# The norm's gain and bias applied to the residual by GpSimd instead of VectorE, at six of seven norms

## The chip, the cores and the metric

The kernel runs on one core of a Trainium2 chip. The metric is device time in microseconds (us) of one execution, as the median over runs. The engines are TensorE (PE, its weight loads PEld), VectorE (DVE), ScalarE (ACT), GpSimd (POOL) and SyncE (SP, which here only starts transfers). All arithmetic is in float32.

## The reference

A first block (gated linear attention, latent attention, a mixture of 64 experts) gives x, of 256 tokens by 1024 features. The change lies in the second block, of two layers, and in the final norm of the first one:

```python
def layer_norm(x, g, b):
    xf = x.astype(jnp.float32)
    mu = jnp.mean(xf, -1, keepdims=True)
    var = jnp.mean(jnp.square(xf - mu), -1, keepdims=True)
    y = (xf - mu) * lax.rsqrt(var + LN_EPS)
    return (y * g.astype(jnp.float32) + b.astype(jnp.float32)).astype(x.dtype)

def second_block(x, mem, ln_g, ln_b, ...):
    alpha = DEEPNORM_ALPHA
    for l in range(DEPTH_2):                      # 2 layers
        x = layer_norm(alpha * x + 0.5 * swiglu(x, ffn_w_gate[l, 0], ffn_w_up[l, 0], ffn_w_down[l, 0]),
                       ln_g[l, 0], ln_b[l, 0])
        ...                                       # u = x @ w_in; tok = short conv (l = 0) or mLSTM (l = 1)
        xa = memory_cross_attention(u[..., -D_XA:], mem_kv)
        mix = jnp.concatenate([tok, xa], -1) @ w_out[l]
        x = layer_norm(alpha * x + mix, ln_g[l, 1], ln_b[l, 1])
        x = layer_norm(alpha * x + 0.5 * swiglu(x, ffn_w_gate[l, 1], ffn_w_up[l, 1], ffn_w_down[l, 1]),
                       ln_g[l, 2], ln_b[l, 2])
    return x
```

So there are seven norms in a row: norm 0 is the RMS norm at the end of the first block (a gain, no bias), norms 1 to 6 are the layer norms (gain g and bias b, each a row of 1024).

## The kernel before

The second block runs as FFN 0, conv, FFN 1, FFN 2, lstm, FFN 3; FFN n works on the result of norm 0, 2, 3 and 5, `conv` on that of norm 1, `lstm` on that of norm 4, and norm 6 ends the kernel. The residual h lies in SBUF as `c_h`: 128 partitions (tokens) by 2 tiles by 1024 features. Each engine runs a program written out by hand, in the order of its functions, and waits for the others by semaphores; there is no scheduler. SyncE loads the weights in 1 MB pieces into a ring of 8 (`x_ring`).

At norm j, VectorE adds the new products from PSUM to h (`sums` L1678, or `merged` L1722 to L1769), takes the statistics, and `scaled(j, t)` (L1684 to L1687; for norm 0 L2040 to L2043) turns tile t of h into (h - mean) / root in place, in two halves of 512 columns, each counted on the semaphore `zn`. TensorE then transposes the tile (`turn`, L1256, semaphore `turned`, four counts a norm), and `spread` moves it from PSUM to `xT`, features by tokens: VectorE does half (L1695, L1697), ScalarE the other (L1563, L1565). The gain and bias are applied there, per feature, as scalars; so TensorE's operand `xT` needs nothing from what follows.

The residual itself also needs gain and bias before the next norm adds to it. `rows(j)` does this on h in place: for each tile a product with `n_g` (L1708; L1711 at norm 0) and, from norm 1 on, an addition of `x_b` (L1709), each 128x1024. `n_g` and `x_b` hold the rows g and b in all partitions; ScalarE's queue reloads them (`load_rows(j)`) behind the semaphore `rows`, at the start of `conv` and `lstm` and in the third step of each FFN. In an FFN VectorE calls `rows(j)` behind `hidden(0)`, the first of 11 steps; in `conv` and `lstm` it is its first work.

An FFN on VectorE starts with `token_sums` (L1802 to L1806): four combinations of quarters of `xT`, all in SBUF. TensorE, which has meanwhile multiplied the plain products of two steps (`plain(0)`, then `turn(j, 1)`, then `plain(1)`), waits for them before `mixed(0)`:

```python
                turn(j, 0)
                ...
                plain(0)
                turn(j, 1)
                plain(1)
                pe.wait_ge(s["tx"], n + 1)
                mixed(0)
```

GpSimd builds constants at the start of the kernel, masks the attention and multiplies a gate (L827) before 101 us, and then works only in `lstm`: two masks and, at L2064, the product of the output gate `x_og` with `x_hg`, two instructions of 128x768.

Of the kernel before, what the change touches and what calls it, by code (L numbers as in the profile page):

```python
# [8 lines left out]
ALU = mybir.AluOpType  # L9
# [7 lines left out]
TT = S // P  # L17
# [1151 lines left out]
def whole(K, M, E, N, X, Y, out):  # L1169
# [38 lines left out]
    with nc.Block() as block:  # L1208
# [459 lines left out]
        def _(v):  # L1668
            c = lambda i: K.vc(v, i)

            def sums(j, t, scale, last):
                for m in range(2):
                    if 2 * t + m < 3:
                        v.wait_ge(s["bank"], BANK_AT[j] + 2 * t + m + 1)
                    else:
                        v.wait_ge(s["spent"], last)
                    hm = h[:, t, m * 512:(m + 1) * 512]
                    c(v.scalar_tensor_tensor(out=hm, in0=yb(t, m), scalar=scale, in1=hm, op0=ALU.mult, op1=ALU.add))  # L1678
                    c(v.bn_stats(N.stats[:, t, m, :], hm))
                v.bn_aggr(N.mv[:, t, :], N.stats[:, t, :, :]).then_inc(s["mv"], 1)  # L1680
# [30 lines left out]
                        v.tensor_tensor(h[:, t, :], h[:, t, :], N.g[:, :], ALU.mult).then_inc(s["rows"], 1)  # L1711

            def norm(j, scale, last):
                sums(j, 0, scale, last)
                scaled(j, 0)
                sums(j, 1, scale, last)
                spread(j, 0)
                scaled(j, 1)
                spread(j, 1)

            def merged(n, j, scale, last):
                add = lambda t, m, x: K.vc.mark(v.scalar_tensor_tensor(out=h[:, t, m * 512:(m + 1) * 512], in0=x, scalar=scale,  # L1722
                                                                       in1=h[:, t, m * 512:(m + 1) * 512], op0=ALU.mult, op1=ALU.add))
                after = lambda n: v.wait_ge(K.vc.sem, n)
                got = lambda n: v.wait_ge(s["bank"], BANK_AT[j] + n)
                prod = lambda p: ps[:, DB[p], :]
                stats = lambda t, m: v.bn_stats(N.stats[:, t, m, :], h[:, t, m * 512:(m + 1) * 512])
                both = lambda o, x, y: K.vc.mark(v.tensor_tensor(N.ud[:, o, :], x, y, ALU.add))
                v.wait_ge(s["kept"], (NFC + 1) * (n + 1))
                x = add(0, 0, N.pd[:, :])  # L1730
                got(2)
                after(x)
                c(add_last(0, 0, prod(2), scale))
                stats(0, 0)
                got(3)
                u2 = both(0, N.pd[:, :], prod(6))
                got(4)
                after(u2)
                u4 = both(1, N.ud[:, 0, :], prod(5))
                y = add(1, 0, N.ud[:, 0, :])  # L1740
                after(u4)
                x = add(0, 1, N.ud[:, 1, :])
                z = add(1, 1, N.ud[:, 1, :])
                got(5)
                after(x)
                c(add_last(0, 1, prod(3), scale))
                c(stats(0, 1))
                v.bn_aggr(N.mv[:, 0, :], N.stats[:, 0, :, :]).then_inc(s["mv"], 1)
                got(6)
                after(z)  # L1750
                z = add(1, 1, prod(7))
                scaled(j, 0)
                y = add(1, 0, prod(7))
                after(z)
                stats(1, 1)
                v.wait_ge(s["spent"], last)
                after(y)
                c(add_last(1, 0, prod(4), scale))
                c(stats(1, 0))
                v.bn_aggr(N.mv[:, 1, :], N.stats[:, 1, :, :]).then_inc(s["mv"], 1)  # L1760
                if j < 6:
                    spread(j, 0)
                scaled(j, 1)
                if j < 6:
                    spread(j, 1)
# [42 lines left out]
            def ffn(n, j):  # L1808
                at = AT_FFN[n]

                def post(cc):
                    v.wait_ge(s["spent"], at + 2 * cc + 2)
                    if n or cc:
                        v.wait_ge(s["post"], NFC * n + cc)
                    if cc >= 2:
                        v.wait_ge(s["act"], NFC * n + cc - 1)
                        v.wait_ge(s["hid"], NFC * n + cc - 1)
                    base = 4 if cc % 2 == 0 else 0
                    prod = lambda p: ps[:, base + GU[p][0], GU[p][1]:GU[p][1] + 256].rearrange("p (w t) -> p w t", w=2)
                    u = lambda i: N.us[:, i, :, :]  # L1820
                    o = lambda f2, t: N.cb[:, cc % 2, 2 * f2 + t, :, :]
                    v.wait_ge(s["kept"], (NFC + 1) * n + cc + 1)
                    one = N.p1[:, cc % 2, :, :]
                    u2 = K.vc.mark(v.tensor_tensor(u(0), one, prod(6), ALU.add))  # L1824
                    v.tensor_tensor(o(0, 0), one, prod(2), ALU.add)
                    v.wait_ge(K.vc.sem, u2)
                    u3 = K.vc.mark(v.tensor_tensor(u(1), u(0), prod(7), ALU.add))
                    u4 = K.vc.mark(v.tensor_tensor(u(2), u(0), prod(5), ALU.add))
                    v.wait_ge(K.vc.sem, u3)
                    v.tensor_tensor(o(1, 1), u(1), prod(5), ALU.add)  # L1830
                    v.wait_ge(K.vc.sem, u4)
                    v.tensor_tensor(o(0, 1), u(2), prod(3), ALU.add)
                    v.tensor_tensor(o(1, 0), u(1), prod(4), ALU.add).then_inc(s["post"], 1)

                def hidden(cc):
                    v.wait_ge(s["act"], NFC * n + cc + 1)
                    v.tensor_tensor(N.hT[:, cc, :, :], N.act[:, cc % 2, :, :], N.cb[:, cc % 2, :, 1, :], ALU.mult).then_inc(s["hid"], 1)

                def hidden_sums(cc):
                    v.wait_ge(s["hid"], NFC * n + cc + 1)  # L1840
                    if cc >= 4:
                        v.wait_ge(s["spent"], at + 2 * NFC + cc - 3)
                    o, x = N.hs[:, cc % 4], N.hT[:, cc]
                    first = K.vc.mark(v.tensor_tensor(o[:, 0], x[:, 1], x[:, 3], ALU.add))
                    v.tensor_tensor(o[:, 2], x[:, 0], x[:, 1], ALU.subtract)
                    v.wait_ge(K.vc.sem, first)
                    c(v.tensor_tensor(o[:, 1], o[:, 0], x[:, 0], ALU.subtract))
                    v.tensor_tensor(o[:, 3], x[:, 2], o[:, 1], ALU.subtract).then_inc(s["hsum"], 1)

                token_sums(n, j)  # L1850
                weight_sums(n, 2)
                weight_sums(n, 3)
                for cc in range(NFC):
                    post(cc)
                    weight_sums(n, 2 * cc + 4)
                    weight_sums(n, 2 * cc + 5)
                    hidden(cc)
                    if cc == 0:
                        rows(j)
                    if cc >= NFC - 2:  # L1860
                        for m in range(2):
                            hidden_sums(2 * (cc - NFC + 2) + m)
                for cc in range(4, NFC):
                    weight_sums(n, 2 * NFC + cc)
                    hidden_sums(cc)
                if n == 1:
                    weight_sums(2, 0)
                    weight_sums(2, 1)
                merged(n, j + 1, 0.5 / ALPHA, at + FPOS)
# [22 lines left out]

            def conv():
                at = AT_CONV
                rows(1)
                c(v.memset(X.pad[:, :, 0:QE], 0.0))
                queries(0, 0, at)

# [29 lines left out]

            def lstm():
                at = AT_LSTM  # L1930
                rows(4)
                queries(1, 1, at)
                v.memset(X.va[:, :, :, HD:HD + 1], 1.0)
                for hh in range(HH):
# [119 lines left out]
        @block.gpsimd  # L2054
        def _(g):
            front.gpsimd(g)
            g.wait_ge(ls["wt"], TT * HH)
            g.affine_select(out=X.wt[:, 0, :, 0:P], in_=X.wt[:, 0, :, 0:P], compare_op=ALU.is_ge, fill=0.0, base=0,
                            pattern=[[0, HH], [1, P]], channel_multiplier=-1).then_inc(ls["masked"], 1)
            g.affine_select(out=X.wt[:, 1, :, P:S], in_=X.wt[:, 1, :, P:S], compare_op=ALU.is_ge, fill=0.0, base=0,  # L2060
                            pattern=[[0, HH], [1, P]], channel_multiplier=-1).then_inc(ls["masked"], 1)
            g.wait_ge(ls["og"], 3)
            for t in range(TT):
                i = g.tensor_tensor(X.og[:, t, :], X.og[:, t, :], X.hg[:, :], ALU.mult)  # L2064
            i.then_inc(ls["ogg"], 1)


def place(nc, into, prefix, at, end, **shapes):
# [138 lines left out]
```

## Time and profile before

| | |
|---|---|
| median of 3 runs | 2252.16 us (2251.8 to 2252.19) |
| profiled execution | 2251.79 us, of which span 2249.9 us |
| TensorE busy | 1843.9 us, 82% |
| VectorE busy | 859.9 us, 38%, 1804 instructions |
| ScalarE busy | 214.2 us, 10% |
| GpSimd busy | 17.9 us, 1%, 41 instructions |

The span is the time between the first and the last record of the profiled execution; the device time is a little longer. The first 1113 us are the first block and the experts; the second block is what follows. PEclk is the clock granted to TensorE as a share of 2.4 GHz: 1.00 is that level and 0.50 is 1.2 GHz.

### The profile page before, as it was taken

How to read it: one execution, taken by the hardware profiler on the slowest of the kernel's cores; microseconds unless marked ns; L12 is line 12 of the kernel's file. 1: busy time of each engine (PE TensorE's matmuls, PEld its weight loads, DVE VectorE, ACT ScalarE, POOL GpSimd, SP SyncE). 2: the span in 40 equal slices, each digit the busy share in tenths (PEclk: the TensorE clock that was granted, in tenths of full speed). 3: DMA queues.
4: the chain of work that ended last, by engine and by line, in shares of the span. 5: the costliest groups of instructions: out<-in, count | busy, mean ns of one | idle time of the engine just before them, and what ended most of it. 6: DMA issues, size and time to landing. Idle time of an engine off the chain costs nothing.

```text
span 2249.9 us, 26172 instructions
## 1 busy us (share of the span) xinstructions
PE 1843.9 (82%) x11372; PEld 1225.0 (54%) x11372; DVE 859.9 (38%) x1804; ACT 214.2 (10%) x409; POOL 17.9 (1%) x41
## 2 busy tenths in 40 slices
PE   8997665566665556656699999999999999989997
PEld 6754232222222222212399658699579947859973
DVE  2223111111011111110276742476776755347675
ACT  2321000000000000000100011000010002201000
POOL 1100000000000000000000000000000000000000
PEclk9998887888887888777899999999999999999999
DMA  9268999999999999999955443365545444315540
GB/s 275 71 244 346 427 427 428 427 428 428 428 424 428 427 428 428 428 428 427 361 173 182 174 160 122 118 200 184 172 150 180 177 150 150 113 59 185 181 186 27
DMA packets 185419, 604.64 MB, mean 269 GB/s; under 512 B 17805, under 2 KB 139079, under 8 KB 161239
## 3 DMA queue, kind: packets, MB, share of 16 engines
q1 hardware_dynamic: 179680, 595.51, 68.4%
q10 hardware_dynamic: 5623, 7.42, 1.0%
q8 instruction: 92, 1.51, 0.3%
q14 instruction: 24, 0.20, 0.0%
HBM read 601.86 MB, written 1.05 MB: 268 GB/s over the span
## 4 chain that ended last, share of the span: by engine, by line
PE 62%; DMA 30%; SPq 3%; DVE 3%; issue 1%; ACT 1%; ACTq 0%; DVEq 0%
PE banks L1280 24%; PE banks L1307 11%; DMA e_W<-in_expert_w_up 10%; DMA e_W<-in_expert_w_down 10%; DMA e_W<-in_expert_w_gate 9%; PE banks L907 6%; PE banks L1355 5%; PE banks L915 3%; PE banks L1399 2%; PE banks L1475 2%; PE banks L203 2%; SPq L144 1%; SPq L887 1%; DMA x_ring<-in_ffn_w_up 1%; PE banks L398 1%
## 5 line engine op out<-in xcount | busy, mean ns | idle before, releaser
L907 PE MATMUL banks<-e_W,e_xT 128*32 128x512 f32 x2048 | 284.8, 716 | 176.5 <-DMA e_W<-in_expert_w_up 87.6
L907 PEld LDWEIGHTS banks<-e_W,e_xT 128*32 128x32 f32 x2048 | 79.4, 129 | 370.0 <-issue 368.7
L915 PE MATMUL banks<-e_W,e_hT 128*32 128x512 f32 x960 | 139.2, 745 | 140.0 <-DMA e_W<-in_expert_w_down 140.0
L1280 PE MATMUL banks<-x_xs,x_sums 128*128 128x128 f32 x2112 | 243.0, 275 | 0.0
L1280 PEld LDWEIGHTS banks<-x_xs,x_sums 128*128 128x128 f32 x2112 | 239.4, 192 | 0.0
L1280 PE MATMUL banks<-x_xT,x_ring 128*128 128x128 f32 x1408 | 169.0, 280 | 8.5 <-DVE x_xT L1695 6.8
L1280 PEld LDWEIGHTS banks<-x_xT,x_ring 128*128 128x128 f32 x1408 | 164.9, 196 | 9.5 <-DVE x_xT L1695 7.5
L915 PEld LDWEIGHTS banks<-e_W,e_hT 128*32 128x32 f32 x960 | 38.2, 133 | 230.3 <-issue 230.3
L1083 DVE TENSOR_TENSOR c_h<-c_h,banks 128x1024 f32<-128x1024 f32 x32 | 39.0, 1221 | 312.3 <-PE banks L935 312.3
L1307 PE MATMUL banks<-x_sums,x_hs 128*128 128x512 f32 x264 | 125.0, 592 | 0.0
L1355 PE MATMUL banks<-x_xT,x_ring 128*128 128x256 f32 x544 | 122.0, 386 | 1.6 <-DVE x_xT L1695 1.6
L1079 DVE TENSOR_TENSOR e_xT<-banks,e_fng 128x512 f32<-128x512 f32 x32 | 20.6, 686 | 255.5 <-PE banks L895 255.5
L1355 PEld LDWEIGHTS banks<-x_xT,x_ring 128*128 128x128 f32 x544 | 104.7, 194 | 17.4 <-DVE x_xT L1695 1.9
L1107 DVE TENSOR_TENSOR e_hid<-e_act,banks 128x512 f32<-128x512 f32 x16 | 11.0, 688 | 234.7 <-PE banks L907 234.7
L1280 PE MATMUL banks<-x_xT,x_sums 128*128 128x128 f32 x704 | 86.2, 276 | 2.6 <-DVE x_xs L1806 2.6
L1280 PE MATMUL banks<-x_xs,x_ring 128*128 128x128 f32 x704 | 85.8, 275 | 0.0
L1307 PEld LDWEIGHTS banks<-x_sums,x_hs 128*128 128x128 f32 x264 | 50.2, 190 | 63.1 <-issue 63.1
L1280 PEld LDWEIGHTS banks<-x_xT,x_sums 128*128 128x128 f32 x704 | 82.1, 192 | 3.4 <-DVE x_xs L1806 3.4
L1280 PEld LDWEIGHTS banks<-x_xs,x_ring 128*128 128x128 f32 x704 | 82.1, 192 | 0.0
L1307 PE MATMUL banks<-x_ring,x_hT 128*128 128x512 f32 x176 | 81.4, 592 | 0.0
L1824 DVE TENSOR_TENSOR x_us<-x_p,banks 128x256 f32<-128x256 f32 x44 | 18.5, 421 | 156.3 <-PE banks L1280 156.3
L935 PE MATMUL banks<-e_y,e_mixT 128*128 128x512 f32 x128 | 59.2, 605 | 18.3 <-ACT e_y L1048 17.1
(466 smaller groups left out, 2027.5 us busy)
## 6 DMA issues: line engine op xcount, KB each, us to landing
e_W<-in_expert_w_gate SPq DMA_DIRECT2D x64, 2048.0 KB, 21.7
e_W<-in_expert_w_up SPq DMA_DIRECT2D x64, 2048.0 KB, 20.7
e_W<-in_expert_w_down SPq DMA_DIRECT2D x64, 2048.0 KB, 20.2
x_ring<-in_ffn_w_gate SPq DMA_DIRECT2D x44, 1024.0 KB, 5.4
x_ring<-in_ffn_w_up SPq DMA_DIRECT2D x44, 1024.0 KB, 7.6
x_ring<-in_ffn_w_down SPq DMA_DIRECT2D x44, 1024.0 KB, 5.1
x_ring<-in_w_in_mlstm SPq DMA_DIRECT2D x13, 1024.0 KB, 5.2
x_ring<-in_w_in_conv SPq DMA_DIRECT2D x10, 1024.0 KB, 5.2
```

The lines of the kernel that those rows point to most:

```text
L144: sp.dma_start(dst, src).then_inc(ld["params"], 16)
L203: i = pe.matmul(o, lhs(k), rhs(k), start=(k == 0), stop=(k == KD - 1))
L398: pe.matmul(ps[:, 4 + 2 * t + n, :], M.yT[:, k, t * P:(t + 1) * P], K.wout[:, k, n * 512:(n + 1) * 512], start=(k == 0), stop=False)
L907: i = pe.matmul(ps[SLOT * j:SLOT * (j + 1), b, :], E.xT[:, x, k, SLOT * j:SLOT * (j + 1)], E.W[:, slot0 + j, k * DE:(k + 1) * DE], start=( ...
L915: i = pe.matmul(ps[SLOT * j:SLOT * (j + 1), 2 + c, :], E.hT[:, f, SLOT * j:SLOT * (j + 1)], E.W[:, slot0 + j, f * D + c * 512:f * D + (c + ...
L935: i = pe.matmul(ps[:, 6 - 2 * t + c, :], E.mixT[:, x, t, :], E.y[:, c * 512:(c + 1) * 512], start=True, stop=True)
L1083: return v.tensor_tensor(K.h[:, t, :], K.h[:, t, :], ps[:, 6 - 2 * t:8 - 2 * t, :].rearrange("p b n -> p (b n)"), ALU.add)
L1280: mm = pe.matmul(ps[:, bank, lo + which * P:lo + (which + 1) * P], a, b, start=(k == 0), stop=(k == 3))
L1307: mm = pe.matmul(ps[:, DB[p], :], a, b, start=(c == 0), stop=(c == NFC - 1))
L1355: mm = pe.matmul(ps[:, bank, f2 * S:(f2 + 1) * S], w8(i)[:, k, f2 * P:(f2 + 1) * P], N.xT[:, k, :], start=(k == 0), stop=(k == KD - 1))
L1399: mm = pe.matmul(yb(t, m), X.mixT[:, 2 * kk + k2, t * P:(t + 1) * P], w2(at + n)[:, k2, m * 512:(m + 1) * 512], start=(n == 0 and k2 == 0) ...
L1475: mm = pe.matmul(ps[:, bank, t * FC:(t + 1) * FC], N.xT[:, k, t * P:(t + 1) * P], w8(i)[:, k, :], start=(k == 0), stop=(k == KD - 1))
```

## The change

The function `rows(j)` of norms 0 to 5 moves from VectorE's program to GpSimd's. VectorE keeps only `rows(6)`. GpSimd runs `rows(0)` to `rows(4)` one after the other behind its last instruction of the first block, each tile as soon as `turned` says that both its halves are transposed and `ld_rows` that g and b are there; then the masks and the product of `lstm`; then `rows(5)`. A chain semaphore (`p_chain`) stands between product and addition of a tile. VectorE waits for the semaphore `rows` before its first addition of the next norm.

```diff
--- before.py
+++ after.py
@@ -1711,6 +1711,7 @@
                         v.tensor_tensor(h[:, t, :], h[:, t, :], N.g[:, :], ALU.mult).then_inc(s["rows"], 1)
 
             def norm(j, scale, last):
+                v.wait_ge(s["rows"], TT * j)
                 sums(j, 0, scale, last)
                 scaled(j, 0)
                 sums(j, 1, scale, last)
@@ -1727,6 +1728,7 @@
                 stats = lambda t, m: v.bn_stats(N.stats[:, t, m, :], h[:, t, m * 512:(m + 1) * 512])
                 both = lambda o, x, y: K.vc.mark(v.tensor_tensor(N.ud[:, o, :], x, y, ALU.add))
                 v.wait_ge(s["kept"], (NFC + 1) * (n + 1))
+                v.wait_ge(s["rows"], TT * j)
                 x = add(0, 0, N.pd[:, :])
                 got(2)
                 after(x)
@@ -1855,8 +1857,6 @@
                     weight_sums(n, 2 * cc + 4)
                     weight_sums(n, 2 * cc + 5)
                     hidden(cc)
-                    if cc == 0:
-                        rows(j)
                     if cc >= NFC - 2:
                         for m in range(2):
                             hidden_sums(2 * (cc - NFC + 2) + m)
@@ -1892,7 +1892,6 @@
 
             def conv():
                 at = AT_CONV
-                rows(1)
                 c(v.memset(X.pad[:, :, 0:QE], 0.0))
                 queries(0, 0, at)
 
@@ -1928,7 +1927,6 @@
 
             def lstm():
                 at = AT_LSTM
-                rows(4)
                 queries(1, 1, at)
                 v.memset(X.va[:, :, :, HD:HD + 1], 1.0)
                 for hh in range(HH):
@@ -2054,6 +2052,19 @@
         @block.gpsimd
         def _(g):
             front.gpsimd(g)
+
+            def rows(j):
+                g.wait_ge(moe.ld_rows, 16 + 32 * j)
+                for t in range(TT):
+                    g.wait_ge(s["turned"], 4 * j + 2 * t + 2)
+                    if j:
+                        K.pc(g, g.tensor_tensor(h[:, t, :], h[:, t, :], N.g[:, :], ALU.mult))
+                        g.tensor_tensor(h[:, t, :], h[:, t, :], N.b[:, :], ALU.add).then_inc(s["rows"], 1)
+                    else:
+                        g.tensor_tensor(h[:, t, :], h[:, t, :], N.g[:, :], ALU.mult).then_inc(s["rows"], 1)
+
+            for j in range(5):
+                rows(j)
             g.wait_ge(ls["wt"], TT * HH)
             g.affine_select(out=X.wt[:, 0, :, 0:P], in_=X.wt[:, 0, :, 0:P], compare_op=ALU.is_ge, fill=0.0, base=0,
                             pattern=[[0, HH], [1, P]], channel_multiplier=-1).then_inc(ls["masked"], 1)
@@ -2063,6 +2074,7 @@
             for t in range(TT):
                 i = g.tensor_tensor(X.og[:, t, :], X.og[:, t, :], X.hg[:, :], ALU.mult)
             i.then_inc(ls["ogg"], 1)
+            rows(5)
 
 
 def place(nc, into, prefix, at, end, **shapes):
```

On VectorE at the start of `conv` (`c_h` is the residual, `n_g` and `x_b` the rows of gain and bias, `n_lnT` the parameters by feature) stood, after norm 1's scaling of tile 1:

```order
L1684 RECIPROCAL n_root<-n_root 128x1
L1687 TENSOR_SCALAR c_h<-c_h,n_mv,n_root 128x512 x2
L1695 TENSOR_SCALAR x_xT<-banks,n_lnT 128x128 x4
L1708 TENSOR_TENSOR c_h<-c_h,n_g 128x1024
L1709 TENSOR_TENSOR c_h<-c_h,x_b 128x1024
L1708 TENSOR_TENSOR c_h<-c_h,n_g 128x1024
L1709 TENSOR_TENSOR c_h<-c_h,x_b 128x1024
L1896 MEMSET x_pad 128x12x3
L1874 COPY x_qx<-banks 64x2x256
```

and now stands:

```order
L1684 RECIPROCAL n_root<-n_root 128x1
L1687 TENSOR_SCALAR c_h<-c_h,n_mv,n_root 128x512 x2
L1695 TENSOR_SCALAR x_xT<-banks,n_lnT 128x128 x4
L1895 MEMSET x_pad 128x12x3
L1874 COPY x_qx<-banks 64x2x256
```

The four instructions on h are gone from VectorE; the order of the others is the same.

On GpSimd (`r_e` and `r_off` are constants of the router, the last work of the first block; the part in brackets is what an instruction waits for) the new instructions stand between that and the masks of `lstm`; these are the first rows of the new piece, those of norms 0 and 1, and norms 2 to 4 repeat the last four:

```order
L835 CAST r_e_187<-r_e32i 128x64 [waits p_chain]
L836 TENSOR_SCALAR r_off<-r_e_187 128x64 [waits p_chain]
L2064 TENSOR_TENSOR c_h<-c_h,n_g 128x1024 [waits s_turned,e_ld_rows]
L2064 TENSOR_TENSOR c_h<-c_h,n_g 128x1024 [waits s_turned]
L2061 TENSOR_TENSOR c_h<-c_h,n_g 128x1024 [waits s_turned,e_ld_rows]
L2062 TENSOR_TENSOR c_h<-c_h,x_b 128x1024 [waits p_chain]
L2061 TENSOR_TENSOR c_h<-c_h,n_g 128x1024 [waits s_turned]
L2062 TENSOR_TENSOR c_h<-c_h,x_b 128x1024 [waits p_chain]
```

GpSimd has 22 more instructions (67 rows where there were 45), and nothing of its own stands ahead of them between norms.

## Rows read from the trace of the kernel before

**Rows 1.** The page: busy time, share of the span and instructions of TensorE

```profile
PE 1843.9 (82%) x11372; PEld 1225.0 (54%) x11372; DVE 859.9 (38%) x1804; ACT 214.2 (10%) x409; POOL 17.9 (1%) x41
```

**Rows 2.** The chain that ended last, FFN 0: start us, us, what

```profile
1126.56 130.69 PE banks L1280 x1168
...
1257.25 63.53 PE banks L1307 x148
```

**Rows 3.** The products of `rows` on VectorE, one line: count, min/median/max ns, forms

```profile
L1708 DVE TENSOR_TENSOR c_h<-c_h,n_g x12: 1211/1218/1220, 1329.3 to 2244.4; 128x1024 f32<-128x1024 f32 x12
```

**Rows 4.** Busy time in a stretch of FFN 2; engine, us busy (instructions), clock, DMA

```profile
1672.00:1688.00 16.00, 16.00 (x145) 16.00 (x145) 15.83 (x27) 1.65 (x3) 0.00 (x0) 1.00 0.72 230
```

**Rows 5.** Timeline at norm 1 and the start of `conv`

```profile
1324.26 1.50 ACT L1563 ACTIVATE x_xT<-banks,n_lnT 128x128 f32<-128x128 f32 x4 [4.03 <-PE banks L1256]
...
1326.70 1.00 DVE L1687 TENSOR_SCALAR c_h<-c_h,n_mv,n_root 128x512 f32<-128x512 f32 x2
...
1330.06 23.76 PE L1355 MATMUL banks<-x_xT,x_ring 128*128 128x256 f32 x96 [1.64 <-DVE x_xT L1695]
```

**Rows 6.** GpSimd and VectorE at 1991.7 us in the LSTM, and line L2017

```profile
1991.71 1.80 POOL L2064 TENSOR_TENSOR x_og<-x_og,x_hg 128x768 f32<-128x768 f32 x1
...
1991.76 1.87 DVE L2017 TENSOR_SCALAR x_pad<-x_pad,x_hmv,x_hrs 128x192 f32<-128x192 f32 x1
...
L2017 DVE TENSOR_SCALAR x_pad<-x_pad,x_hmv,x_hrs x8: 366/368/1871, 1991.8 to 1995.3; 128x192 f32<-128x192 f32 x8
```

**Rows 7.** Timeline at 94 to 98 us: start, us, engine, line, operation

```profile
94.83 1.89 POOL L827 TENSOR_TENSOR q_rg<-q_rg,w_gg 128x1024 f32<-128x1024 f32 x1 [14.54 <-ACT q_rg L531]
...
95.64 0.42 DVE L664 TENSOR_TENSOR q_st<-q_st,banks 128x256 f32<-128x256 f32 x1
...
96.10 0.90 DVE L665 TENSOR_TENSOR q_st<-q_st,w_dec 128x256 f32<-128x256 f32 x1
...
97.49 0.43 DVE L665 TENSOR_TENSOR q_st<-q_st,w_dec 128x256 f32<-128x256 f32 x1
```

**Rows 8.** Timeline at the start of FFN 0

```profile
1113.38 0.88 DVE L2043 TENSOR_SCALAR c_h<-c_h,n_root 128x512 f32<-128x512 f32 x2
...
1113.68 1.14 ACT L1565 ACTIVATE x_xT<-banks,n_lnT 128x128 f32<-128x128 f32 x4 [0.54 <-PE banks L1256]
...
1115.35 6.38 PE L1280 MATMUL banks<-x_xT,x_ring 128*128 128x128 f32 x32 [1.71 <-DVE x_xT L1697]
...
1122.64 0.37 ACT L1565 ACTIVATE x_xT<-banks,n_lnT 128x128 f32<-128x128 f32 x1 [7.81 <-PE banks L1256]
...
1123.88 0.69 DVE L1802 TENSOR_TENSOR x_xs<-x_xT 128x512 f32<-128x512 f32 x1 [0.56 <-ACT x_xT L1565]
```

**Rows 9.** Timeline at the start of FFN 2

```profile
1649.02 1.50 ACT L1563 ACTIVATE x_xT<-banks,n_lnT 128x128 f32<-128x128 f32 x4 [4.03 <-PE banks L1256]
...
1651.42 3.84 PE L1280 MATMUL banks<-x_xT,x_ring 128*128 128x128 f32 x32 [2.44 <-DVE x_xT L1695]
...
1651.47 1.00 DVE L1687 TENSOR_SCALAR c_h<-c_h,n_mv,n_root 128x512 f32<-128x512 f32 x2
...
1656.17 1.51 ACT L1563 ACTIVATE x_xT<-banks,n_lnT 128x128 f32<-128x128 f32 x4 [5.46 <-PE banks L1256]
...
1657.78 0.69 DVE L1802 TENSOR_TENSOR x_xs<-x_xT 128x512 f32<-128x512 f32 x1 [0.68 <-ACT x_xT L1563]
...
1658.39 0.68 DVE L1803 TENSOR_TENSOR x_xs<-x_xT 128x512 f32<-128x512 f32 x1
...
1660.45 2.05 PE L1280 MATMUL banks<-x_xT,x_sums 128*128 128x128 f32 x16 [0.75 <-DVE x_xs L1806]
```

**Rows 10.** Busy time and granted clock around norm 1 and in FFN 2

```profile
1323.00:1330.00 7.00, 2.33 (x17) 1.63 (x15) 6.60 (x17) 3.19 (x9) 0.00 (x0) 0.92 1.07 342
...
1330.00:1333.00 3.00, 2.94 (x7) 2.44 (x8) 2.93 (x4) 0.00 (x0) 0.00 (x0) 0.50 0.79 246
...
1655.50:1660.40 4.90, 4.21 (x38) 4.01 (x36) 3.95 (x9) 3.45 (x7) 0.00 (x0) 1.00 0.36 111
```

## The prediction

> **What bounds the kernel now.** I read the page first: TensorE is busy 82% of the span [rows 1]. Then the chain of waits. In the part that the change touches (from 1113 us, after the expert layer) it consists of long unbroken runs of matmuls: one FFN is 130.69 us of products at L1280 and 63.53 us at L1307, with nothing between [rows 2]. Only at the norms does the chain leave TensorE, for a few microseconds each: additions, scaling, transposes, the spread into xT, and `token_sums`. The question is therefore whether the 22 moved instructions lie on these short crossings or under the long runs, before and after.
>
> **What the change removes: nothing from the path.** VectorE loses 22 instructions of about 1.22 us [rows 3], 26.8 us of busy time. Those of norms 0, 2, 3 and 5 stood behind `hidden(0)`, inside an FFN. In FFN 2's stretch around them TensorE is busy 16.00 of 16.00 us while VectorE is also nearly full (15.83) [rows 4]; the other three FFNs read the same. VectorE is full there, but TensorE does not wait for it, so an earlier VectorE is worth 0. Those of norms 1 and 4 stood at the head of `conv` and `lstm`, in the time in which TensorE works on its first 96 matmuls (23.76 us from 1330.06 [rows 5]); again 0. If the cover were gone, each norm would be worth 4 x 1.22 = 4.9 us, but no row shows TensorE waiting for them.
>
> **The new wait is free.** `rows(j)` must be done before norm j+1's first addition. GpSimd needs some 10 us from the transposes; the next addition is far behind that: an FFN is 194 us, and the first 96 matmuls of `conv` alone are 23.76 us [rows 2, 5]. ScalarE's reload of g and b waits for GpSimd too, ahead of `conv` and `lstm`, but its next work is after the second or later group of matmuls. 0 us.
>
> **What the change adds: GpSimd on the path of VectorE.** On GpSimd, one product of two real 128x768 operands took 1.80 us [rows 6]. In proportion 128x1024 is 1.80 x 1024/768 = 2.40 us. The lower bound is the 1.89 us of L827 on 128x1024, whose second operand repeats one column per block [rows 7]; I take 2.40, because both operands of the moved work are full rows.
> [...]
>
> More important is when it runs. Before, the instructions stood deep in the FFN. Now GpSimd has nothing else to do and starts as soon as the transposes of a tile are done, which is when ScalarE's spread starts. That is exactly the crossing. And these two rows show that the engines exclude each other:
> - L2017 on VectorE, one SBUF operand into SBUF, normally 0.368 us, took 1.871 us: it began at 1991.76 beside the GpSimd product of 1991.71 to 1993.51, and ended at 1993.63, 0.12 us after it [rows 6].
> - L665, two SBUF operands, took 0.90 instead of 0.43 us beside the GpSimd product of 94.83 to 96.72, and ended at 97.00. L664, with one operand in PSUM, ran beside the same product in its normal 0.42 us [rows 7].
>
> So VectorE's SBUF-only instructions stand still until GpSimd's ends; those that read PSUM don't. A stopped one ends 0.12 to 0.28 us after the release (192 and 256 elements; 0.55 us for 512, by proportion of the second).
> The Trainium skill (SBUF — State Buffer, section "SBUF: two separate sides") calls it an exclusive lock held for a whole instruction by whichever began first; the trace agrees in both rows. It does not say who is next when GpSimd waits and VectorE has its next instruction ready; that is the choice below.
>
> Now each crossing. The SBUF-only instructions of VectorE there are `scaled` (L1687, L2043) and `token_sums` (L1802 to L1806).
> 1. **FFN 0, second tile's scaling.** Tile 0 is transposed at 1113.68. L2043's two halves of tile 1 run 1113.38 to 1114.26 in the order of the program ahead of the spread [rows 8]. GpSimd's product takes the port behind the first of them (about 1113.9) and ends at 1116.3; the second half ends at 1116.5 instead of 1114.26: **+2.3 us**, and all of it is on the path, since the spread and TensorE's start at 1115.35 stand behind it.
> 2. **conv and lstm, tile 1's scaling.** Tile 0's product starts at 1324.3 and ends at 1326.7, as L1687 begins (1326.70). Whoever gets the port first, GpSimd's addition (2.40 us) goes ahead of at least the second half, and the tile's transposes, its spread and the matmuls at 1330.06 stand behind both halves [rows 5]. **+2.3 us**, and the same in the norm ahead of `lstm`, whose rows repeat this pattern: together +4.6. Tile 1's two GpSimd instructions end before VectorE next needs SBUF alone.
> 3. **Tile 1's scaling in FFN 1, 2, 3: hidden.** In FFN 2 tile 0 is transposed at 1649.02, the product runs 1649.1 to 1651.5, L1687 starts at 1651.47, the addition goes between its halves to 1654.4. The transposes that need it come behind the first 32 matmuls, which end at 1655.26 [rows 9]. They are the cover; 0 us, with under a microsecond to spare.
> 4. **`token_sums` behind tile 1's product.** FFN 2: tile 1 is transposed at 1656.17, the product ends at 1658.6. L1802 is ready at 1657.78 and ends at 1659.15 instead of 1658.47: +0.7, and TensorE's 1660.45 waits for these four [rows 9]. Three such FFNs: **+2.1**. FFN 0: transposed at 1122.64, product to 1125.0, L1802 ready at 1123.88, +1.0 [rows 8]. Together **+3.1**.
> 5. **`token_sums` behind tile 1's addition.** GpSimd asks for the port again 0.1 to 0.2 us later, while L1802 runs. If it gets it next, L1803 stands still for 2.4 us. FFN 1, 2, 3: **+7.2**; FFN 0 has no addition.
>
> Sum: 2.3 + 4.6 + 3.1 + 7.2 = **17.2 us**.
>
> **The clock.** After the gaps around the transposes at 1323 to 1330 us (TensorE busy 2.33 of 7.00) the granted clock is 0.50, the 1.2 GHz level, for 3 us [rows 10]. The price of such a fall is in the first 32 matmuls of an FFN: 6.38 us in FFN 0, which starts behind a like gap, and 3.84 us in FFN 2 [rows 8, 9], so 2.5 us. At FFN 2's `token_sums` TensorE is busy 4.21 of 4.90 us and the clock stays at 1.00, the 2.4 GHz level [rows 10]. With 3 us more idle there, each of four such places may fall: 0 to 10.2 us. I take one, 2.5 us.
>
> **Forecast.** 17.2 + 2.5 = 19.7 us, on the profiled execution's 2251.79 us (span 2249.9 and 1.9 around it), which is 0.4 under the median 2252.16: **2272 us**, 0.9% slower.
>
> **Rivals.**
> - *VectorE keeps the port while its next instruction is ready* (not slower). Records of back-to-back VectorE instructions overlap by 0.08 us (L1802 runs 1657.78 to 1658.47, L1803 starts at 1658.39) [rows 9], so the port may never come free between them. Then items 1, 2 and 5 vanish and only item 4 is left: +3.1 us, 2255.3 us. It decides at the first L2043 pair. For it: these overlaps. Against: L1805 and L1806 wait for a semaphore of the instruction before them. 0.15. A difference under 0.2% (4.5 us) is what a measurement of this kernel can't tell from no change, so this counts as the same.
> - *Every collision and every fall of the clock*: 17.2 + 10.2 = 27.4 us, 2280 us. For it: each lengthened gap resembles the one at 1323 us. 0.12.
> - *No cost*: GpSimd wakes late enough to miss the crossings, or the norm waits for something else meanwhile; 2252 us. It would have to wake over 7 us late (from 1649.0 past 1655.3 or from 1656.2 past `token_sums`), and nothing in the trace shows such a delay. 0.05.
> - *Faster*: VectorE's 4.9 us per FFN free TensorE after all. It would need a TensorE wait there, and [rows 4] has none; one FFN's worth of it would give 2247 us. 0.03.
> - The forecast with no, one or two falls of the clock: 0.65.
>
> **Range and chances.** The forecast and the second rival are slower, 0.77; the first rival plus a single fall of the clock would also pass 4.5 us, so slower 0.79, same 0.18, faster 0.03. With 1.89 instead of 2.40 us for a GpSimd instruction, the sum is some 5 us smaller (0.51 us at each of the ten collisions), which lies in between. The range takes in the first rival's 2255 and reaches past the second's 2280: 2255 to 2282. The forecast's own range is 2266 to 2278.
>
> **What would show it.** GpSimd: 22 more instructions, about 2.4 us, the first at 1113.7. VectorE: single records of L2043, L1687 and the `token_sums` lines of 2 to 3 us; the norm's crossings longer, the FFN runs of 130.69 and 63.53 us unchanged. If all `token_sums` records are 0.69 us except the first, the first rival holds. I would be wrong above all if the lock were won by VectorE each time, or if GpSimd's records themselves grew to several times 2.4 us because they are the ones that wait.

## The result, and the profile after

The changed kernel takes 2275.2 us (median of 4 runs, 2270.92 to 2276.73) against 2252.18 us: ratio 1.0101, 95% interval [1.0088, 1.0113]. It is 23 us slower. The profiled execution took 2273.82 us, with a span of 2272.0 us, 22.1 us over the span before. In what follows one execution of one kernel (GpSimd's work on other data) took 2856.6 us at a mean granted clock of 0.638 and is left out; all others of a kernel lie within 0.2% of its median.

The page of the changed kernel, busy time by engine, to be set beside [rows 1]:

```profile
PE 1850.8 (81%) x11372; PEld 1230.1 (54%) x11372; DVE 856.9 (38%) x1782; ACT 214.2 (9%) x409; POOL 70.5 (3%) x63
```

VectorE has lost 22 instructions of 1.22 us, 26.8 us, and yet is busy only 3.0 us less (859.9 before). So its other instructions have records that are some 24 us longer in all. Which ones, the view by line of the changed kernel says (count, then min/median/max ns):

```profile
L2041 DVE TENSOR_SCALAR c_h<-c_h,n_root x4: 479/486/2642, 1112.0 to 1113.8; 128x512 f32<-128x512 f32 x4
...
L1687 DVE TENSOR_SCALAR c_h<-c_h,n_mv,n_root x24: 535/545/2715, 1324.1 to 2263.6; 128x512 f32<-128x512 f32 x24
...
L1804 DVE TENSOR_TENSOR x_xs<-x_xT x4: 1341/1344/1703, 1125.3 to 2056.7; 128x512 f32<-128x512 f32 x4
...
L1805 DVE TENSOR_TENSOR x_xs<-x_xT x4: 680/2826/2827, 1127.0 to 2058.0; 128x512 f32<-128x512 f32 x4
...
L1807 DVE TENSOR_TENSOR x_xs<-x_xT,x_xs x4: 678/679/680, 1127.6 to 2060.7; 128x512 f32<-128x512 f32 x4
```

L2041 and L1687 are the scaling, L1804 to L1808 the four instructions of `token_sums` (L1802 to L1806 before). The first of `token_sums` takes at least 1.34 us instead of 0.69 in every FFN, the second 2.83 us in three of four, and the third always its own time. The timeline of the changed kernel at the starts of FFN 0, `conv` and FFN 1 shows why:

```profile
1113.39 3.04 DVE L2041 TENSOR_SCALAR c_h<-c_h,n_root 128x512 f32<-128x512 f32 x2
1113.69 1.14 ACT L1565 ACTIVATE x_xT<-banks,n_lnT 128x128 f32<-128x128 f32 x4 [0.54 <-PE banks L1256]
1113.81 2.34 POOL L2064 TENSOR_TENSOR c_h<-c_h,n_g 128x1024 f32<-128x1024 f32 x1 [1012.89 <-PE banks L1256]
...
1117.52 5.65 PE L1280 MATMUL banks<-x_xT,x_ring 128*128 128x128 f32 x32 [3.87 <-DVE x_xT L1697]
...
1326.82 2.35 POOL L2061 TENSOR_TENSOR c_h<-c_h,n_g 128x1024 f32<-128x1024 f32 x1 [200.34 <-PE banks L1256]
1326.88 0.69 DVE L1728 BATCH_NORM_STATS2 n_stats<-c_h 128x6 f32<-128x512 f32 x1
...
1329.16 3.16 DVE L1687 TENSOR_SCALAR c_h<-c_h,n_mv,n_root 128x512 f32<-128x512 f32 x2
1329.24 2.34 POOL L2062 TENSOR_TENSOR c_h<-c_h,x_b 128x1024 f32<-128x1024 f32 x1
...
1335.53 23.06 PE L1355 MATMUL banks<-x_xT,x_ring 128*128 128x256 f32 x96 [1.64 <-issue]
...
1451.87 2.36 POOL L2061 TENSOR_TENSOR c_h<-c_h,n_g 128x1024 f32<-128x1024 f32 x1 [1.99 <-PE banks L1256]
...
1453.43 1.34 DVE L1804 TENSOR_TENSOR x_xs<-x_xT 128x512 f32<-128x512 f32 x1 [0.68 <-ACT x_xT L1563]
...
1454.30 2.67 POOL L2062 TENSOR_TENSOR c_h<-c_h,x_b 128x1024 f32<-128x1024 f32 x1
1454.70 2.83 DVE L1805 TENSOR_TENSOR x_xs<-x_xT 128x512 f32<-128x512 f32 x1
1457.45 0.68 DVE L1807 TENSOR_TENSOR x_xs<-x_xT,x_xs 128x512 f32<-128x512 f32 x1
...
1458.91 3.48 PE L1280 MATMUL banks<-x_xT,x_sums 128*128 128x128 f32 x16 [3.55 <-DVE x_xs L1808]
```

Read the FFN 1 part slowly. GpSimd's product ends at 1454.23; L1804, ready since 1453.43, ends at 1454.77, 0.54 us later. The addition has asked for the port at 1454.30, and its record is 2.67 us instead of 2.34, since it first waits for L1804. L1805 begins at 1454.70, ends at 1457.53, again 0.56 us behind the addition (1456.97). So each side gets the port (the way to SBUF that the two engines are taken to share) when the other's instruction ends, although VectorE had its next instruction ready. TensorE waits 3.55 us for `token_sums`, against 0.75 before; [rows 9] show the same place in FFN 2. At `conv` the two halves of the scaling take 3.16 instead of 1.00 us together [rows 5], and in FFN 0 3.04 instead of 0.88 [rows 8]. At `conv` it is the first half that is stopped: its record begins at 1329.16, the product ends at 1329.17, the addition runs from 1329.24 to 1331.58, and the first half ends at 1331.87, after 2.71 us. The second half takes its usual time. So the addition went ahead of an instruction whose record had begun 0.08 us earlier.

One line of the `conv` part limits the reading. The statistics (L1728) take their only input from the residual in SBUF and write to SBUF, and yet took their usual 0.69 us in the middle of GpSimd's product (1326.82 to 1329.17). So "SBUF-only" is too wide a name for what stands still: held up here are the scaling and the instructions with two operands in SBUF.

The second cost shows as a lower clock. The chain of the changed kernel has the same long runs as [rows 2], but those of FFN 1, 2 and 3 have grown from 130.69 to 132.32 us:

```profile
1129.02 130.69 PE banks L1280 x1168
1259.71 63.53 PE banks L1307 x148
...
1458.91 132.32 PE banks L1280 x1168
1591.22 63.53 PE banks L1307 x148
```

Windows of the changed kernel around FFN 1's `token_sums` (us, then PE, PEld, DVE, ACT, POOL busy, granted clock, DMA) say that it is the granted clock, which is 1.00 up to the gap and 0.56 behind it:

```profile
1453.50:1458.90 5.40, 1.86 (x17) 1.66 (x15) 5.37 (x5) 1.77 (x3) 3.40 (x2) 1.00 0.00 0
1458.90:1462.00 3.10, 3.09 (x16) 3.10 (x17) 3.07 (x6) 0.00 (x0) 0.00 (x0) 0.56 0.00 0
```

Following the chain of both kernels from crossing to crossing gives the whole account:

| crossing | collision, us | clock, us | shift so far, us |
|---|---|---|---|
| FFN 0: scaling; `token_sums` | 2.2; 1.0 | -0.7 (first 32 matmuls 5.65 instead of 6.38) | 2.5 |
| conv: scaling | 2.3 (see below) | | 4.8 |
| FFN 1: `token_sums` | 2.8 | 1.6 (long run) | 9.2 |
| FFN 2: `token_sums` | 2.8 | 1.6 (first 32, 5.46 instead of 3.84), 1.6 (long run) | 15.3 |
| lstm: scaling | 2.3 | | 17.6 |
| FFN 3: `token_sums` | 2.8 | 1.6 (long run) | 22.1 |

That is 16.2 us of collisions and 5.7 us of clock; rounding hides another 0.2 us. The 2.3 us at `conv` are a net figure: the first half of the scaling ends 2.2 us later, the transposes and the spread behind it take 0.9 us more at a lower clock, and the 96 matmuls win back 0.7 us (23.06 instead of 23.76).

The clock column has two parts that differ in what they prove. The 1.6 us in the long runs of FFN 1, 2 and 3 (4.9 us) stand behind gaps lengthened by `token_sums`, from 0.75 to 3.55 us. The 1.6 us in FFN 2's first 32 matmuls don't: the gap ahead of them is 2.44 us in both kernels. They took 5.47 us, too, in two kernels below that have no collision there and are no slower (`late` and `tail_product`, whose FFN 3 in turn took 3.84 us where the kernel before has 5.47). So this part isn't shown to be the change's doing, and neither is the 0.7 us won back in FFN 0.

### The profile page after: what moved, and what is told of

Read it like the earlier page. It is cut to its first block, busy times and chain, and to the rows that moved or that the text cites. A ratio compares the mean times of both kernels' runs of the same rounds, so it can differ in the third digit from the quotient of the medians.

```text
span 2272.0 us, 26178 instructions
## 1 busy us (share of the span) xinstructions
PE 1850.8 (81%) x11372; PEld 1230.1 (54%) x11372; DVE 856.9 (38%) x1782; ACT 214.2 (9%) x409; POOL 70.5 (3%) x63
## 4 chain that ended last, share of the span: by engine, by line
PE 62%; DMA 30%; DVE 4%; SPq 3%; issue 1%; ACT 1%; ACTq 0%; DVEq 0%
PE banks L1280 24%; PE banks L1307 11%; DMA e_W<-in_expert_w_up 10%; DMA e_W<-in_expert_w_down 10%; DMA e_W<-in_expert_w_gate 9%; PE banks L907 6%; PE banks L1355 5%; PE banks L915 3%; PE banks L1399 2%; PE banks L1475 2%; PE banks L203 2%; SPq L144 1%; SPq L887 1%; DMA x_ring<-in_ffn_w_up 1%; PE banks L398 1%
```

## The experiments

Eight kernels ran. They stand beside runs of the kernel before on the same chip: 2252.0 us (median of 18) for the first four, 2251.69 us (of 33) for the others. Those runs lie between 2249.88 and 2254.28 us, a wider spread than in the result above; part of it comes from ahead of the norms, where nothing differs, since the first scaling starts anywhere from 1110.5 to 1113.8 us in the profiled executions. My theory: VectorE's scaling and its instructions with two operands in SBUF exclude GpSimd's, and are excluded by them, and the change put GpSimd's into the crossings, where VectorE's are on the path. The rivals: GpSimd's work costs in proportion wherever it is; the order and the new semaphores of the residual cost.

**Only tile 0 by GpSimd.** VectorE keeps tile 1 where it was.

```diff
+                for t in (0,):                      # GpSimd's rows(j), j < 6
+                    g.wait_ge(s["turned"], 4 * j + 2 * t + 2)
...
-                for t in range(TT):                 # VectorE's rows(j)
+                for t in (range(TT) if j == 6 else (1,)):
```

> GpSimd takes only tile 0 of each moved norm; VectorE keeps tile 1 at its old place. If each collision is an SBUF-only VectorE instruction standing still behind a GpSimd instruction, only the scaling of tile 1 is hit: 2.2 us in FFN 0 and 2.3 us each at conv and lstm, 6.8 us in all, with 0 to 3 us of clock more or less: 2257 to 2262 us. The records of token_sums are 0.69 us. Rival, that the cost comes from all of GpSimd's work alike (half of it here): +11.5 us, 2263.7 us.

2259.16 us, +7.2 us, ratio 1.0031 [1.0021, 1.0041]. By line:

```profile
L1687 DVE TENSOR_SCALAR c_h<-c_h,n_mv,n_root x24: 535/546/2717, 1319.7 to 2245.5; 128x512 f32<-128x512 f32 x24
...
L1804 DVE TENSOR_TENSOR x_xs<-x_xT x4: 692/694/694, 1122.0 to 2043.0; 128x512 f32<-128x512 f32 x4
```

The scaling is hit and `token_sums` not at all. But only two of the three scalings are hit. In FFN 0 the pair of halves was over at 1112.75, and GpSimd's product began at 1113.00: the transposes of tile 0, which release it, took 1.81 us there, at a granted clock of 0.57, against 1.09 us at 1.00 in the changed kernel. Item 1 is thus a race that, in these two traces, the speed of the transposes decides, by a few tenths of a microsecond. The 7.2 us are two scalings of 2.3 us, 4.6 us, and 2.6 us that these don't account for. The profiled execution, at 2255.77 us, is one of the two shortest of nine (2255.62 to 2261.28) and shows 5.5 us, counted from tile 1's scaling in FFN 0 to the end; whether the race went the other way in the longer ones isn't known.

**Only tile 1 by GpSimd.** The mirror image, with `(1,)` for GpSimd and `(0,)` for VectorE.

> GpSimd takes only tile 1; VectorE keeps tile 0. Port theory: only token_sums are hit, 1.0 us in FFN 0 and 2.8 us in each of FFN 1, 2, 3, 9.4 us; the granted clock falls behind the lengthened gaps, 1.6 us each in three FFNs, 4.9 us: +14.3 us, 2266 us, and every record of the scaling is 0.54 us. The two halves together make the 22 us of the change. Rival, that the halves are alike: +11.5 us each. If the clock falls whatever the gap before token_sums, it is in tile0_only too.

2265.96 us, +14.0 us, ratio 1.0061 [1.0044, 1.0078].

```profile
L1687 DVE TENSOR_SCALAR c_h<-c_h,n_mv,n_root x24: 540/544/549, 1322.3 to 2257.1; 128x512 f32<-128x512 f32 x24
...
L1804 DVE TENSOR_TENSOR x_xs<-x_xT x4: 1404/1408/1779, 1123.5 to 2050.2; 128x512 f32<-128x512 f32 x4
...
L1805 DVE TENSOR_TENSOR x_xs<-x_xT x4: 679/2824/2828, 1125.2 to 2051.5; 128x512 f32<-128x512 f32 x4
```

Every scaling has its own time, and the four `token_sums` are within 0.1 us of the changed kernel's. The three long runs behind them took 132.32, 132.32 and 132.27 us. The same number of GpSimd instructions costs twice what tile 0's do: it is the place that counts, not only the amount. The two halves add up to 21.2 us, against 23 for the change.

**The same work on other data.** VectorE does all rows as before; GpSimd does two-operand instructions of 128x1024 on the memory values, which nobody writes, into a scratch tile.

```diff
+            def other(j):
+                for t in range(TT):
+                    g.wait_ge(s["turned"], 4 * j + 2 * t + 2)
+                    K.pc(g, g.tensor_tensor(X.bin[:, :], mv[:, :], mv[:, :], ALU.mult))
+                    if j:
+                        K.pc(g, g.tensor_tensor(X.bin[:, :], mv[:, :], mv[:, :], ALU.add))
```

> The kernel before, with VectorE still doing all rows, and GpSimd doing two-operand instructions of 128x1024 at the moments of the change on operands that no other engine touches at that time (it reads the memory values, writes a scratch tile in bfloat16; the output is the reference's). Port theory: the crossings are as in the changed kernel, +22 us, 2271 to 2277 us. Rival, that the residual itself (its order, its semaphore, the new waits of VectorE and ScalarE) makes the cost: 2252 us.

2264.31 us (median of three: 2264.18, 2264.31 and, profiled, 2268.42), +12.3 us, ratio 1.0055 [1.0035, 1.0076]. The rival (2252 us) falls: without any change to the residual, its waits or VectorE's program, over half of the loss is there. It is less than the +22 us I expected, and the trace says in part why:

```profile
1327.16 1.90 POOL L2063 TENSOR_TENSOR x_bin<-c_memv 128x1024 bf16<-128x1024 f32 x1 [200.34 <-PE banks L1256]
```

My stand-in takes 1.90 us, not 2.35, so each collision is shorter (the longest scaling 2.06 instead of 2.72 us, the second of `token_sums` 2.37 instead of 2.83). And TensorE's gap at `token_sums` is 2.69 us in FFN 1, 2 and 3 alike, but only FFN 2's long run grew to 132.32 us; the other two kept their 130.69. So what the clock did behind a gap of that length was not always the same.

**The same work later.** In an FFN GpSimd waits for the fourth `hidden`, in `conv` and `lstm` for the spread of both tiles. ScalarE's reload of gain and bias moves with it.

```diff
                     g.wait_ge(s["turned"], 4 * j + 2 * t + 2)
+                    if j in AT_NORM:                 # [0, 2, 3, 5]
+                        g.wait_ge(s["hid"], NFC * AT_NORM.index(j) + 4)
+                    else:
+                        g.wait_ge(s["xt_v"], TT * (j + 1))
+                        g.wait_ge(s["xt_a"], TT * (j + 1))
...
-                    if c == 2:                       # ScalarE, in an FFN
+                    if c == 7:
                         load_rows(j + 1)
```

> The changed kernel, with GpSimd released later: in an FFN behind the fourth hidden, in conv and lstm behind the spread of both tiles; ScalarE's reload of gain and bias in an FFN moves from its third to its eighth step. Port theory: nothing SBUF-only of VectorE on the path collides; inside the FFN TensorE covers: 2252 us, at most +3 if VectorE, held up for up to 9.4 us in each FFN, is late for a product. Rival, that the work on GpSimd costs wherever it stands (waits, memory): still +10 us or more.

2252.65 us, ratio 1.0004 [0.9994, 1.0013]: no difference. All 22 instructions are still GpSimd's. A window of FFN 1 in which its four run, and the scaling by line:

```profile
1500.00:1512.00 12.00, 12.00 (x110) 12.00 (x109) 7.57 (x12) 1.02 (x2) 9.73 (x4) 1.00 0.55 171
```

```profile
L1688 DVE TENSOR_SCALAR c_h<-c_h,n_mv,n_root x24: 539/544/548, 1320.3 to 2240.8; 128x512 f32<-128x512 f32 x24
```

TensorE is busy in 12.00 of 12.00 us beside GpSimd's 9.73. This is the whole change without its place in time. It also agrees with VectorE's 26.8 us being worth nothing, though GpSimd holds VectorE up there too (one L1788 in this FFN took 2.85 us instead of 0.68), so it is no test of their removal alone.

**Only the product by GpSimd.** VectorE adds `x_b` at the old place.

```diff
                     if j:
-                        K.pc(g, g.tensor_tensor(h[:, t, :], h[:, t, :], N.g[:, :], ALU.mult))
-                        g.tensor_tensor(h[:, t, :], h[:, t, :], N.b[:, :], ALU.add).then_inc(s["rows"], 1)
+                        g.tensor_tensor(h[:, t, :], h[:, t, :], N.g[:, :], ALU.mult).then_inc(s["mulled"], 1)
```

> GpSimd makes only the products of norms 0 to 5, at the moments of the change; VectorE makes the additions at their old place. Port theory with GpSimd let in between two VectorE instructions: the scaling in FFN 0 is hit by 2.2 us; at conv and lstm the product ends as the scaling begins, 0 to 0.1 us; token_sums stand behind the product alone, 1.0 us in FFN 0 and 0.65 us in each of the other three. +5.2 us and one clock fall at most: 2257 to 2259 us. Rival, that half the GpSimd work is half the cost: +11 us or more.

2258.38 us, +6.7 us, ratio 1.0026 [1.0017, 1.0035]. At `conv` the tie is as narrow as expected and costs nothing; its timeline:

```profile
1326.29 2.34 POOL L2068 TENSOR_TENSOR c_h<-c_h,n_g 128x1024 f32<-128x1024 f32 x1 [200.34 <-PE banks L1256]
...
1328.63 1.00 DVE L1687 TENSOR_SCALAR c_h<-c_h,n_mv,n_root 128x512 f32<-128x512 f32 x2
```

The product ends at 1328.63, exactly where L1687 begins. Left are FFN 0's scaling and the first of each `token_sums` (1.34 us, 1.71 in FFN 0), 5.1 us in all, and the clock. So most of the change's loss hangs on the ten additions, each of which asks for the port right behind a product. Of the clock, the chain of waits shows two things, in FFN 1 and at FFN 2's start:

```profile
1443.68 5.46 PE banks L1280 x32
...
1454.98 130.69 PE banks L1280 x1168
...
1655.08 5.47 PE banks L1280 x32
```

Behind the less lengthened `token_sums` the long run has its 130.69 us, and so have the other three. But the first 32 matmuls of FFN 1 and FFN 2 lost 1.6 us each (3.84 before), again behind gaps as long as before (2.18 and 2.44 us).

**Writes only.** VectorE does all rows; GpSimd fills a scratch tile, four times a tile of the residual, without reading anything.

```diff
+                    for _ in range(4 if j else 2):
+                        K.pc(g, g.memset(X.bin[:, :], 0.0))
```

> The kernel before, with VectorE doing all rows, and GpSimd writing zeros to a scratch tile (no operand read) at the moments of the change, four writes a tile (two at norm 0). If a GpSimd instruction holds VectorE's second port whatever it does, both the scaling and token_sums have records over their own time, each by up to one write of about 1 us: +5 to 12 us, 2257 to 2264 us. If what is fought over in token_sums is the reading of two operands alone, the token_sums stay at 0.69 us, only the scaling (one operand, 0.54 us) is longer: +1 to +5 us. If only reads collide at all: 2252 us.

2254.63 us, +2.9 us, ratio 1.0012 [1.0003, 1.0022]. By line:

```profile
L1687 DVE TENSOR_SCALAR c_h<-c_h,n_mv,n_root x24: 540/546/1247, 1321.9 to 2245.1; 128x512 f32<-128x512 f32 x24
...
L1802 DVE TENSOR_TENSOR x_xs<-x_xT x4: 691/692/693, 1124.1 to 2042.6; 128x512 f32<-128x512 f32 x4
```

The middle case: a write of GpSimd (about 1 us each) holds up the scaling, which has one operand (up to 1.25 instead of 0.54 us), and leaves `token_sums`, two operands, entirely alone, although a series of four writes (two in FFN 0) runs beside each. The Trainium skill (SBUF — State Buffer, section "SBUF: two separate sides") limits the collision of a two-operand instruction to a GpSimd instruction that reads SBUF; the trace agrees, with 0.693 us as the longest of four.

**The last norm's tile 0 by GpSimd.** Two attempts at a gain: at norm 6 nothing covers VectorE's rows, 4.8 us, behind which only the output's transfer is left. One gives GpSimd product and addition of tile 0, the other the product alone; all else is the kernel before.

```diff
+            g.wait_ge(moe.ld_rows, 16 + 32 * 6)
+            g.wait_ge(s["zn"], 4 * 6 + 2)
+            K.pc(g, g.tensor_tensor(h[:, 0, :], h[:, 0, :], N.g[:, :], ALU.mult))      # tail_both; .then_inc(s["early"], 1) in tail_product
+            g.tensor_tensor(h[:, 0, :], h[:, 0, :], N.b[:, :], ALU.add).then_inc(s["early"], 1)   # tail_both only
```

> The kernel before, but at the last norm alone GpSimd does product and addition of tile 0 while VectorE is busy with tile 1; VectorE does tile 1 as before. Before, VectorE's four instructions at the end took 4.7 us of the path. GpSimd starts behind tile 0's scaling, 4.7 us before the end of its addition; the second half of tile 1's scaling stands still for about 0.6 us; two instructions (2.4 us) leave the end: 1.7 us faster, about 2250.4 us against 2252.1. Rival: the transfer of tile 0 or GpSimd's addition is late, and nothing is gained.

> The kernel before, but at the last norm GpSimd makes only the product of tile 0, in the time in which VectorE still works from PSUM; it ends before the scaling of tile 1. Nothing collides and one VectorE instruction of 1.2 us leaves the end: 1.2 us faster, about 2250.9 us against 2252.1.

2251.53 us, ratio 0.9998 [0.9989, 1.0007], and 2250.65 us, ratio 0.9995 [0.9986, 1.0004], against 2251.69 us. Neither can be told from no change by the measured times. The timelines of the end can tell more; first product and addition (span 2251.0), then the product alone (span 2248.5):

```profile
2242.26 2.34 POOL L2069 TENSOR_TENSOR c_h<-c_h,x_b 128x1024 f32<-128x1024 f32 x1
...
2243.01 2.33 DVE L1687 TENSOR_SCALAR c_h<-c_h,n_mv,n_root 128x512 f32<-128x512 f32 x2
```

```profile
2237.70 2.35 POOL L2071 TENSOR_TENSOR c_h<-c_h,n_g 128x1024 f32<-128x1024 f32 x1 [243.26 <-DVE c_h L1687]
...
2240.87 1.00 DVE L1687 TENSOR_SCALAR c_h<-c_h,n_mv,n_root 128x512 f32<-128x512 f32 x2
```

From the start of tile 1's scaling to the end of the span it is 8.0 us with both, 7.6 us with the product alone, and 8.85 us before. With both, the addition holds up both halves of the scaling (2.33 instead of 1.00 us), where I had expected 0.6 us for the second half alone, and over half of the 2.4 us saved is lost again. The product alone fits beside instructions that read PSUM and the statistics, and its 1.2 us are saved in full. It is the best version of this study by its trace, at a gain below what the runs resolve.

## Why the prediction was right

- **What is removed is worth 0**: right as far as the traces show. In the changed kernel no long run and no crossing is shorter for it, and `late`, which has the same instructions off VectorE, is no faster.
- **The new wait is free**: right. VectorE's first addition of a norm is never released by GpSimd. At the FFNs it waits for ScalarE's copy `x_pd` in both kernels, idle 24.9 us in four times, and behind `conv` and `lstm` for TensorE, 1.19 and 1.83 us against 1.11 and 1.75 before.
- **GpSimd's instruction, 2.40 us**: measured 2.34 to 2.36 where it isn't itself held up. The Trainium skill (GPSIMD Engine Reference, section on performance versus the Vector engine) gives 4497 ns for an addition of 2048 elements; half of it, an estimate of 2.25 us, is a little low.
- **Items 1, 2 and 3**: 2.2 us measured for 2.3 in FFN 0; 2.3 each for 2.3 at `conv` and `lstm`; hidden in FFN 1 to 3 as said (the two halves of L1687 take 3.04 us at 1447.12 and TensorE's matmuls behind 1447.07 run on). Two things I had not said: item 1 depends on how fast tile 0's transposes run and fell away in `tile0_only`; and at `conv` the addition went ahead of both halves, where I had it at least ahead of the second.
- **Items 4 and 5**: 1.0 for 1.0 in FFN 0; 2.8 for 3.1 (0.7 + 2.4) in the other three. In FFN 1 the addition ends 2.20 us behind L1804 where I had 2.40 us of standing still, and the stopped L1805 then ends 0.56 us behind it instead of needing its full 0.68.
- **Who gets the port**: GpSimd, in each case, between two VectorE instructions. The first rival (VectorE keeps it, 2255 us) is refuted by every L1805 of 2.83 us and by `tile1_only`. Sum of the collisions 16.2 us for 17.2.
- **Which instructions stand still**: the rule "SBUF-only" was too wide. The statistics (L1728) were not held up. They are on the path at `conv` but were not in the sum, so nothing in it changed.
- **The clock**: this term was mis-sized. I took one fall of 2.5 us among the four `token_sums`. There were three, in FFN 1, 2 and 3, of 1.6 us each; the sign that I named, FFN runs unchanged at 130.69 us, failed in three of four. The price was too high, since I had read it from a stretch that began at 0.50, and the number too low. Another 1.6 us at FFN 2's start and the 0.7 us won back at FFN 0 come from places that I hadn't in the term. In all it is 5.7 us for 2.5.
- **The sum**: its two errors, -1.0 and +3.2 us, have opposite signs, and by that luck the total (22.1 us for 19.7, the last 0.2 is rounding) came nearer than the clock term did. The measured median is 3 us above the forecast, with the four executions of the changed kernel 5.8 us apart. One figure of a rival was off, with nothing resting on it: to wake at 1655.3 instead of 1649.0 is 6.3 us late, not over 7.
- **What a measurement can tell**: I had counted differences under 0.2% as none. With ten executions, `writes` (+0.12%) was told apart.

## What to carry to other kernels

Before work is handed to an idle GpSimd, look at when it will start, not only at how long it takes: a wait that is free on the engine that gave the work away can release it into the one stretch where that engine is on the path. On this kernel the same 22 instructions cost 23 us there and nothing measurable when they started about 6 us (`conv`, `lstm`) or 55 to 65 us (FFNs) later. On the path, keep GpSimd's instructions apart from VectorE's with two operands in SBUF and from its scalings from SBUF to SBUF. Beside VectorE instructions that read PSUM, and beside the statistics, they cost nothing here; one that only writes left those with two operands alone.

## What the runs showed of the hardware

- Neither engine starves the other: in FFN 1 GpSimd and VectorE took the port in turn, an instruction each (2.34 us for 0.6 us of VectorE's), even when VectorE's next instruction was ready. Each turn of GpSimd then costs VectorE nearly GpSimd's full length (L1805, 2.83 instead of 0.68 us).
- Not every VectorE instruction that stays in SBUF is held up: the statistics took 0.69 us beside a GpSimd product, as without one.
- The record of a stopped instruction includes its wait, so VectorE's busy time, 859.9 to 856.9 us, hid that it had 26.8 us less work.
- A stopped instruction ends 0.54 to 0.56 us behind the release when it has 512 elements and two operands (0.69 us alone), 0.28 to 0.29 us when it has one operand (0.54 alone). The order is not simply that of the records' starts: at `conv` the VectorE record that began 0.08 us before the addition's still went second.
- GpSimd's two-operand instruction on 128x1024 took 2.35 us on two full rows and 1.90 us when both operands were the same tile and the output bfloat16. Which of the two differences does it was not tried.
- Each gap of 3.5 to 3.6 us at `token_sums` (three in the changed kernel, three in `tile1_only`) was followed by 1.6 us more in the long run; in FFN 1 of the changed kernel the granted clock was 0.56 for the first 3.1 us of it. Of three gaps of 2.69 us (`elsewhere`), one was. Behind equal gaps of 2.44 us FFN 2's first 32 matmuls took 3.84 us in some kernels and 5.47 in others, so the gap just ahead doesn't decide it alone; what else does wasn't tested.
- The changed kernel's runs spread over 5.8 us, those of the kernel before beside them over 0.5. That this is the clock falling in some executions and not in others was not shown.
